# State-space phase: SyncE's u and lag stores ahead of its loads, and a second buffer for the lag kernels' load in place of the fourth unit buffer

## The chip, the cores and the metric

The kernel runs on one core of one Trainium2 chip. The metric is the device time of one execution in microseconds. The kernel before took 1748.19 us, the median of three runs (1745.48 to 1751.16).

## The reference

The kernel computes two blocks of a small model on 256 tokens of width 1024, in float32. The change lies in the second layer of the first block, a state-space mixer (S5) over 2048 channels, cut into 128 groups of 16 channels with 64 complex states each, forward and backward in time:

```
u = p.reshape(tokens, 128 groups, 16)            # p, z: the two halves of h @ s5_w_in
abar = exp(lam * dt);  bbar = ((abar - 1) / lam) * b;  cmat = c
h_t = abar * h_{t-1} + bbar u_t ;  y_t = Re(cmat h_t)     # both directions, first over the 256 context tokens
y = d * u + y_forward + y_backward
out = gelu(y) * sigmoid(gelu(y) @ glu_w + glu_b)          # then * silu(z) @ w_out, and a layer norm
```

## The kernel before

The state-space phase is the function s5_mixer. It works in chunks of 128 channels (8 groups), CT = 16 chunks, software-pipelined over steps n = 0 to 26. The recurrence is cut into pieces of CH = 8 tokens: states are carried from piece to piece by a scan, and inside a piece the effect of u on y is a small convolution, whose matrices (the "lag kernels") are worked out on the chip. In step n, TensorE (PE) does in this order:

- lag_kernels(n-9): ps_l from V and b (L1769 to L1778), then ScalarE copies it to lags (L1899).
- project(n): u of chunk n, 24 matmuls of 512 columns (L1745); from step 16 on a gate_half (24 of 256 columns) in place of it, and a second one at the end of the step. The weights come as "units" of 512 KB, which ScalarE and VectorE first split into a leading part and a rest (lead, L1858; rest, L1971).
- outputs(n-10): y from V and the states hs, and from the lag kernels T and u (L1794).
- the state matmuls of chunk n-2: ps_s from the 1 MB input weights W and the re-laid u, ub (L1841). ScalarE copies them into S (L1936 to L1938).

VectorE scans S in quads of four chunks (advance, L1982 to L1985), spread over steps n = 4q+6 to 4q+9; ScalarE's states() (L1878, L1879) then makes hs. GpSimd (POOL) makes V of a chunk (L1729 to L1731) once the outputs three chunks before are done (y_done), except for chunks 4, 6, 8, 10 and 12, whose V is loaded (quad_loads, L1611).

SyncE issues all of the phase's transfers, in program order, on one queue; a wait on SyncE stops everything behind it. Its loop over n does before:

1. unit load n+4 (512 KB, L1505), after rest(n); from step 16 on two units
2. W load of chunk n-1 (1 MB, L1509), after the state matmuls of chunk n-3
3. u store of chunk n-1 (256 KB, L1646), after u_kept
4. z and g stores and loads (L1650, L1655, L1659)
5. lag store of chunk n-9 (four DMAs of 30 KB, L1663), then b (L1597), cc (L1600) and every fourth step apow (L1606)
6. ub load of chunk n-1 (256 KB, L1680), after the u store has landed (u_stored): it reads u back in another layout
7. T load of chunk n-9 (512 KB, L1688), after the lag store has landed and after outputs(n-10) (y_done): it reads overlapping windows of the lag kernels, 1 KB each
8. V loads, tables, gate weights, and the small loads of the first steps

T has one buffer, half of the resident x (whose contents are spilled for the phase). Units have four buffers in the ring, u % 4. PE waits in outputs(k) for T_landed, in project for the unit (through rest_made), in the state matmuls for s5_w_landed and ub_landed. The DRAM side of the u store has 8 as its outermost count, that of the T and ub loads too, that of one lag store 16, that of the unit, W, b and cc loads 128.

Of the kernel before, what the change touches and what calls it, by code (L numbers as in the profile page):

```python
# [21 lines left out]
P = 128  # L22
DM = 1024
KT = DM // P
NL = 256
# [5 lines left out]
ET = E // P  # L31
# [35 lines left out]
class Core:  # L67


    def __init__(self, nc, ctx, d):  # L70
        self.nc, self.d = nc, d
        sb = lambda name, shape: ctx.enter_context(nc.sbuf_tensor(f"resident_{name}", shape, F32))
        self.ring = sb("ring", [P, 2, KT * NW])
        self.x = sb("x", [P, LT, DM])
        self.ident = sb("ident", [P, P])
        self.modT = sb("modT", [P, 2, 16, 2])
        self.eps = sb("eps", [P, 2])
        self.norm_g = sb("norm_g", [P, 4, KT])
        self.fold = sb("fold", [P, 2, KT])
        self.ms, self.rs = sb("ms", [P, LT, 2]), sb("rs", [P, LT])  # L80
        self.landed = [ctx.enter_context(nc.semaphore(f"weights_landed{s}")) for s in range(2)]
        many = lambda n, c: [ctx.enter_context(nc.semaphore(f"{n}{s}")) for s in range(c)]
        self.s5_unit_landed, self.s5_w_landed, self.gate_landed = many("s5_unit_landed", 4), many("s5_w_landed", 2), many("gate_landed", 4)
        self.q_stored = ctx.enter_context(nc.semaphore("q_stored"))
        self.tables_stored = ctx.enter_context(nc.semaphore("tables_stored"))
        self.spent = []
        self.used = [0, 0]
# [1074 lines left out]
CH = 8  # L1162
# [333 lines left out]
def s5_unit(core, u):  # L1496
    return core.ring[:, 0, (u % 4) * KT * P:(u % 4 + 1) * KT * P]

# [5 lines left out]
def s5_unit_load(core, sp, u):  # L1504
    sp.dma_start(s5_unit(core, u), core.d["s5_w"][u]).then_inc(core.s5_unit_landed[u % 4], 16)  # L1505

# [5 lines left out]
def s5_prefetch(core, sp):  # L1512

    for u in range(4):
        s5_unit_load(core, sp, u)
    for k in range(2):
        s5_weights_load(core, sp, k)
# [10 lines left out]
def s5_mixer(core, hparts, xc, low, wparts, gT):  # L1528
# [6 lines left out]
    with phase(core, "ssm") as ph:  # L1535
# [21 lines left out]
        vt = ph.sb("vt", [P, 512])  # L1557
        T = core.x[:, 0, :].rearrange("p (j m q) -> p j m q", j=4, q=2)
        yv = core.x[:, 1, :].rearrange("p (t m) -> p t m", t=CH)
# [9 lines left out]
        y_done, y_kept, turned, g_made, cleared, feed_made = [sem(n) for n in "y_done y_kept turned g_made cleared feed_made".split()]  # L1569
        lag_stored, T_landed, g_stored, z_stored, feed_in = [sem(n) for n in "lag_stored T_landed g_stored z_stored feed_in".split()]  # L1570
        ub_landed = [sem(f"ub_landed{s}") for s in range(3)]
# [14 lines left out]
        def windows(k):  # L1586

            return bass.AP(tensor=lagged.tensor, offset=lagged.offset + k * SG * CG * LAGW, ap=[[2 * SG, CH], [2 * LAGW, SG * 4], [1, 2 * P]])

        with ph.block() as block:  # L1590
            @block.sync
            def _(sp):
# [41 lines left out]
                for n in range(STEPS + 1):  # L1634
                    k, kl = n - OUT, n - LAG
                    for u in units(n):
                        if u + 4 < SsmUnits.UNITS:
                            sp.wait_ge(rest_made, u + 1)
                            s5_unit_load(core, sp, u + 4)
                    if n >= 3 and is_ct(n - 1):  # L1640
                        sp.wait_ge(s_done, 2 * (n - 2))
                        s5_weights_load(core, sp, n - 1)
                    if is_ct(n - 1):
                        sp.wait_ge(u_kept, n)
                        to = d["u"][n - 1]
                        sp.dma_start(bass.AP(tensor=to.tensor, offset=to.offset, ap=[[CH * NCH, CG], [CG * CH * NCH, SG], [1, CH * NCH]]), us[(n - 1) % 2][:]).then_inc(u_stored[(n - 1) % 2], 16)  # L1646
                    done = units(n - 1)
                    if done and done[0] >= CT:
# [7 lines left out]
                    if k in (6, 10):  # L1656
                        q = (k - 6) // 4
                        sp.wait_ge(g_made, 2 * (q + 1))
                        sp.dma_start(d["g"][4 * q:4 * q + 4].rearrange("j p n -> p j n"), gb[:]).then_inc(g_stored, 16)  # L1659
                    if is_ct(kl):  # L1660
                        sp.wait_ge(l_kept, kl + 1)
                        for j in range(4):
                            sp.dma_start(lagged[kl][:, j], lags[32 * j:32 * j + SG].rearrange("m w q -> m (w q)")).then_inc(lag_stored, 16)  # L1663
                        if kl + 2 < CT:
                            sp.wait_ge(l_done, kl + 1)
                            small_loads(kl + 2)
                        if kl + 4 < CT:
                            if kl not in LOADED:
                                sp.wait_ge(v_made, 2 * quads_made(kl))
                            c_load(kl + 4)  # L1670
                    if n >= BACK + 8 and (n - BACK - 8) % 4 == 0 and (n - BACK) // 4 < NQ:
                        sp.wait_ge(scanned, (n - BACK) // 4 - 1)
                        apow_load((n - BACK) // 4)
                    if is_ct(n - 1):
# [10 lines left out]
                    if is_ct(kl):  # L1685
                        sp.wait_ge(lag_stored, 64 * (kl + 1))
                        sp.wait_ge(y_done, kl)
                        sp.dma_start(core.x[:, 0, :].rearrange("p (j m) -> p j m", j=4), windows(kl)).then_inc(T_landed, 16)  # L1688
                    if kl == CT - 2:
                        for u in range(2):  # L1690
                            gate_load(core, sp, u)
                    if is_ct(k) and k + 3 in LOADED:
                        sp.wait_ge(y_done, k + 1)
                        quad_loads(k + 3)
                    if is_ct(k) and k % 4 == 3 and k // 4 + 2 < NQ:
                        sp.wait_ge(v_made, 2 * quads_made(k))
                        table_load(k // 4 + 2)
                    later_loads(n)
                sp.wait_ge(rest_made, SsmUnits.UNITS)
                for u in range(2, 4):  # L1700
                    gate_load(core, sp, u)
                sp.wait_ge(z_stored, 16 * (CT // 2))
# [32 lines left out]
            def _(pe):  # L1735
# [45 lines left out]
                def outputs(k):  # L1781
                    pe.wait_ge(hs_made, k + 1)
                    if k >= 4 and k % 2 == 0:
                        pe.wait_ge(y_kept, k // 2 - 1)
                    pe.wait_ge(T_landed, 16 * (k + 1))
                    pe.wait_ge(ul_made, k + 1)
                    for q in range(2):
                        r = 2 * k + q
                        bank, slot = ps_y[r % 8 // 4], r % 4
                        for src in range(3):  # L1790
                            for j in range(4):
                                lhs = ul[:, k % 9, 4 * q + j, :] if src == 2 else hs[:, src, (r % 8) * 4 + j, :]
                                rhs = T[:, j, :, q] if src == 2 else V[:, r % RING, src, j, :]
                                last = nc.tensor.matmul(bank[32 * j:32 * j + 32, slot, :], lhs, rhs, start=src == 0, stop=src == 2)  # L1794
                    last.then_inc(y_done, 1)
# [21 lines left out]
                for n in range(STEPS):  # L1817
# [3 lines left out]
                    if n < CT:  # L1821
                        pe.wait_ge(core.s5_unit_landed[n % 4], 16 * (n // 4 + 1))
                        pe.wait_ge(u_kept, n)
                        project(n, ps_u[:], slice(0, NTOK), u_done)
# [24 lines left out]
            def _(act):  # L1849
                sc = nc.scalar  # L1850

                def lead(u):
                    act.wait_ge(core.s5_unit_landed[u % 4], 16 * (u // 4 + 1))
                    if u >= 2:
                        act.wait_ge(u_done, min(u - 1, CT))
                        if u - 1 > CT:
                            act.wait_ge(z_done, u - 1 - CT)
                    sc.activation(w_lead[:, u % 2], s5_unit(core, u).rearrange("p (k c) -> p k c", k=KT), ACT.Copy).then_inc(lead_made, 1)  # L1858
# [34 lines left out]
                for n in range(STEPS):  # L1893
                    k, kl = n - OUT, n - LAG
                    if is_ct(kl):
                        if kl:
                            act.wait_ge(lag_stored, 64 * kl)
                        act.wait_ge(l_done, kl + 1)
# [1241 lines left out]
def build(nc, d, out, start=0):  # L3140

    for name, shape in (("mod", [2, 2, DM]), ("s5_q", [SN, CH, 2, P]), ("s5_p", [P, NQ, CH, 2, QG]), ("s5_a", [P, NQ, LEVELS, 3, QG]),
                        ("s5_bb", [P, 2, SN, SG]), ("s5_W", [CT, P, 4, WB * 2 * P]), ("s5_V", [2 * len(EarlyQuads.TILES), P, 2, 4 * P]), ("x1", [P, LT, DM]), ("u", [CT, SG, CG, CH * NCH]),
                        ("lags", [CT, SG, 4, LAGW * 2]), ("g", [ET, P, NL]), ("z", [ET, P, NL])):
        d[name] = nc.dram_tensor(name + "_scratch", shape, F32, kind="Internal").ap()
# [158 lines left out]
```

## Time and profile before

| | us |
|---|---|
| median of three runs (lowest, highest) | 1748.19 (1745.48, 1751.16) |
| span of the profiled execution, first to last instruction | 1745.1 |
| the profiled execution's own time beside its span | not given by the page |
| PE busy in the span | 1558.8 (89%) |
| state-space phase in the trace, about | 562 to 923 |

The page is of one profiled execution. Times in the views are microseconds from the start of the span. An engine's "idle before" is the time it waited ahead of an instruction, with the releaser that came last by the profile; where it says "issue", the profile shows no engine that released it, which for a wait on a DMA's semaphore is the usual form. The granted clock of TensorE is given as a share of full speed (1.00 is 2.4 GHz, 0.50 is 1.2 GHz, a mean over a stretch lies between). The DMA share is the mean busy share of the core's 16 DMA engines.

### The profile page before, as it was taken

How to read it: one execution, taken by the hardware profiler on the slowest of the kernel's cores; microseconds unless marked ns; L12 is line 12 of the kernel's file. 1: busy time of each engine (PE TensorE's matmuls, PEld its weight loads, DVE VectorE, ACT ScalarE, POOL GpSimd, SP SyncE). 2: the span in 40 equal slices, each digit the busy share in tenths (PEclk: the TensorE clock that was granted, in tenths of full speed). 3: DMA queues.
4: the chain of work that ended last, by engine and by line, in shares of the span. 5: the costliest groups of instructions: out<-in, count | busy, mean ns of one | idle time of the engine just before them, and what ended most of it. 6: DMA issues, size and time to landing. Idle time of an engine off the chain costs nothing. (4 is left out here: it accounts for less than half of the span.)

```text
span 1745.1 us, 28068 instructions
## 1 busy us (share of the span) xinstructions
PE 1558.8 (89%) x11286; PEld 1331.2 (76%) x11286; DVE 975.0 (56%) x1271; ACT 806.6 (46%) x1096; POOL 661.1 (38%) x507
## 2 busy tenths in 40 slices
PE   3799999799798888888759988898999999899998
PEld 0378888588686777778658976677999967689997
DVE  6444422488744267556825636564666655546665
ACT  2522222455414557576554434554544454455452
POOL 0088986599698923445751013211000010110000
PEclk9889999899899989889978998888999999899999
DMA  9966666455535567777756545313454433245441
GB/s 390 426 247 224 236 228 229 140 195 192 200 113 197 158 196 209 200 242 191 206 140 254 186 165 206 145 49 146 194 216 170 167 111 136 85 166 217 194 167 49
DMA packets 118649, 330.75 MB, mean 190 GB/s; under 512 B 31732, under 2 KB 72052, under 8 KB 102280
## 3 DMA queue, kind: packets, MB, share of 16 engines
q1 hardware_dynamic: 115670, 303.67, 49.6%
q10 hardware_dynamic: 2868, 25.54, 4.0%
q8 instruction: 78, 1.28, 0.3%
q14 instruction: 33, 0.27, 0.0%
HBM read 290.55 MB, written 38.62 MB: 189 GB/s over the span
## 5 line engine op out<-in xcount | busy, mean ns | idle before, releaser
L3010 PE MATMUL ffn_ps<-ffn_x_lead,w_lead 128*128 128x256 f32 x672 | 188.4, 280 | 1.1 <-DVE w_rest L3089 1.1
L3010 PE MATMUL ffn_ps<-ffn_x_lead,w_rest 128*128 128x256 f32 x672 | 188.6, 281 | 0.0
L3010 PE MATMUL ffn_ps<-ffn_x_rest,w_lead 128*128 128x256 f32 x672 | 188.4, 280 | 0.0
L401 POOL TENSOR_TENSOR w_rest<-resident_ring,w_lead 128x2048 fp32r<-128x2048 f32 x7 | 32.1, 4580 | 402.1 <-ACT w_lead L397 211.7
L3089 DVE TENSOR_TENSOR w_rest<-resident_ring,w_lead 128x2048 fp32r<-128x2048 f32 x42 | 96.1, 2292 | 83.8 <-ACT w_lead L3054 83.8
L365 PE MATMUL qkvz_ps<-qkvz_w_lead,h_lead 128*128 128x512 f32 x320 | 125.7, 393 | 5.4 <-POOL h_rest L646 5.4
L3010 PEld LDWEIGHTS ffn_ps<-ffn_x_lead,w_lead 128*128 128x128 f32 x672 | 126.1, 188 | 2.2 <-issue 1.5
L3010 PEld LDWEIGHTS ffn_ps<-ffn_x_rest,w_lead 128*128 128x128 f32 x672 | 126.4, 188 | 0.7
L3010 PEld LDWEIGHTS ffn_ps<-ffn_x_lead,w_rest 128*128 128x128 f32 x672 | 126.3, 188 | 0.0
L365 PE MATMUL qkvz_ps<-qkvz_w_rest,h_lead 128*128 128x512 f32 x320 | 125.4, 392 | 0.0
L365 PE MATMUL qkvz_ps<-qkvz_w_lead,h_rest 128*128 128x512 f32 x320 | 125.4, 392 | 0.0
L282 DVE TENSOR_TENSOR qkvz_w_rest<-resident_ring,qkvz_w_lead 128x2048 fp32r<-128x2048 f32 x20 | 50.7, 2534 | 124.2 <-ACT qkvz_w_lead L276 124.2
L282 DVE TENSOR_TENSOR w_rest<-resident_ring,w_lead 128x2048 fp32r<-128x2048 f32 x33 | 78.3, 2375 | 73.5 <-ACT w_lead L276 73.1
L1729 POOL TENSOR_TENSOR ssm_V<-ssm_ptab,ssm_cc 128x512 f32<-128x512 f32 x44 | 59.2, 1346 | 140.0 <-PE ssm_ps_y L1794 137.2
L276 ACT ACTIVATE qkvz_w_lead<-resident_ring 128x2048 fp32r<-128x2048 f32 x20 | 38.5, 1924 | 150.2 <-PE qkvz_ps L365 148.0
L1971 DVE TENSOR_TENSOR w_rest<-resident_ring,w_lead 128x1024 fp32r<-128x1024 f32 x32 | 46.9, 1469 | 107.1 <-ACT w_lead L1858 106.9
L276 ACT ACTIVATE w_lead<-resident_ring 128x2048 fp32r<-128x2048 f32 x33 | 63.2, 1914 | 89.6 <-PE odd_ps L365 29.9
L3054 ACT ACTIVATE w_lead<-resident_ring 128x2048 fp32r<-128x2048 f32 x42 | 80.1, 1912 | 50.7 <-PE ffn_ps L3010 50.6
L1418 POOL TENSOR_TENSOR resident_x<-xc,resident_x 128x512 f32<-128x512 f32 x64 | 99.1, 1548 | 5.0
L1745 PE MATMUL ssm_ps_u<-h_lead,w_lead 128*128 128x512 f32 (+1 forms) x256 | 93.8, 366 | 4.6 <-issue 2.4
L1745 PE MATMUL ssm_ps_u<-h_lead,w_rest 128*128 128x512 f32 (+1 forms) x256 | 88.9, 347 | 2.6 <-issue 2.6
L1745 PE MATMUL ssm_ps_u<-h_rest,w_lead 128*128 128x512 f32 (+1 forms) x256 | 89.2, 348 | 0.0
(518 smaller groups left out, 4531.6 us busy)
## 6 DMA issues: line engine op xcount, KB each, us to landing
resident_ring<-in_ffn_gu SPq DMA_DIRECT2D x22, 2048.0 KB, 9.0
ffn_wd<-in_ffn_down SPq DMA_DIRECT2D x22, 1024.0 KB, 4.8
resident_ring<-in_ada_w SPq DMA_DIRECT2D x8, 2048.0 KB, 13.6
xc<-s_q_scratch SPq DMA_DIRECT2D x128, 128.0 KB
resident_x<-in_s_bT SPq DMA_DIRECT2D x64, 256.0 KB
resident_ring<-in_attn_w_in ACTq DMA_DIRECT2D x8, 2048.0 KB, 10.1
s_W_scratch<-resident_x SPq DMA_DIRECT2D x64, 256.0 KB, 3.5
resident_ring<-in_s_w SPq DMA_DIRECT2D x32, 512.0 KB, 6.1
```

The source lines that it names most:

```text
L276: self.core.nc.scalar.activation(self.w[0][j], self.core.tile(r)[:, j * HK:(j + 1) * HK, :], ACT.Copy).then_inc(self.lead_made, 1)
L282: self.core.nc.vector.tensor_tensor(self.w[1][j], self.core.tile(r)[:, j * HK:(j + 1) * HK, :], self.w[0][j].bitcast(F32), ALU.subtract).t ...
L365: last = nc.tensor.matmul(bank(parity, t), self.lhs[x][:, half * HK + k, t * P:(t + 1) * P], self.w[w][j][:, k, :], start=(half, k, x, w) ...
L401: self.core.nc.gpsimd.tensor_tensor(self.slots[1][0], self._raw(r), self.slots[0][0].bitcast(F32), ALU.subtract).then_inc(self.rest_made, 1)
L1418: g.tensor_tensor(b, q(0), b, ALU.mult).then_inc(self.scaled, 1)
L1729: g.tensor_tensor(v, power(c), coef(0), ALU.mult)
L1745: last = nc.tensor.matmul(out, w[:, s, k, :], hparts[x][:, k, cols], start=k == 0 and x == 0 and w is w_lead, stop=k == KT - 1 and w is w_ ...
L1971: v.tensor_tensor(w_rest[:, u % 2], raw, w_lead[:, u % 2].bitcast(F32), ALU.subtract).then_inc(rest_made, 1)
L3010: last = nc.tensor.matmul(ps[s][f][:, m, :], w_part[w][m][:, k, f * P:(f + 1) * P], x_part[x][:, k, :], start=(k, w, x) == (0, 0, 0), stop ...
L3054: nc.scalar.activation(w_part[0][m], raw(s, m), ACT.Copy).then_inc(w_lead_made, 1)
L3089: v.tensor_tensor(w_part[1][m], raw(s, m), w_part[0][m].bitcast(F32), ALU.subtract).then_inc(w_rest_made, 1)
```

## The change

SyncE's loop now runs in this order: u store; from step 16 on the two unit loads; z and g; W load; lag store; ub load; T load; below step 16 the unit load; b, cc and apow; V loads and tables; gate weights. The four lag stores of 16 partitions each become one of all 128 partitions (twice the bytes), and the scratch tensor gets twice the rows, so that the windows read by T are the same. T has two buffers: half of x, and what was the fourth unit buffer; T(k) waits for outputs(k-2) in place of outputs(k-1). Units have three buffers, and each is asked for three units ahead in place of four. T_landed becomes two semaphores. At the end gate load 3, which overwrites the second T buffer, waits for outputs(14).

```diff
 def s5_unit(core, u):
-    return core.ring[:, 0, (u % 4) * KT * P:(u % 4 + 1) * KT * P]
+    return core.ring[:, 0, (u % 3) * KT * P:(u % 3 + 1) * KT * P]
...
-        T = core.x[:, 0, :].rearrange("p (j m q) -> p j m q", j=4, q=2)
+        T_raw = [m.rearrange("p (j m) -> p j m", j=4) for m in (core.x[:, 0, :], core.ring[:, 0, 3 * KT * P:4 * KT * P])]
+        T = [m.rearrange("p j (m q) -> p j m q", q=2) for m in T_raw]
...
                 for n in range(STEPS + 1):
                     k, kl = n - OUT, n - LAG
-                    for u in units(n):
-                        if u + 4 < SsmUnits.UNITS:
-                            sp.wait_ge(rest_made, u + 1)
-                            s5_unit_load(core, sp, u + 4)
-                    if n >= 3 and is_ct(n - 1):
-                        sp.wait_ge(s_done, 2 * (n - 2))
-                        s5_weights_load(core, sp, n - 1)
                     if is_ct(n - 1):
                         sp.wait_ge(u_kept, n)
                         to = d["u"][n - 1]
...
+                    if n >= CT:
+                        for u in units(n):
+                            if u + 3 < SsmUnits.UNITS:
+                                sp.wait_ge(rest_made, u + 1)
+                                s5_unit_load(core, sp, u + 3)
...
+                    if n >= 3 and is_ct(n - 1):
+                        sp.wait_ge(s_done, 2 * (n - 2))
+                        s5_weights_load(core, sp, n - 1)
                     if is_ct(kl):
                         sp.wait_ge(l_kept, kl + 1)
-                        for j in range(4):
-                            sp.dma_start(lagged[kl][:, j], lags[32 * j:32 * j + SG].rearrange("m w q -> m (w q)")).then_inc(lag_stored, 16)
-                        if kl + 2 < CT:
-                            sp.wait_ge(l_done, kl + 1)
-                            small_loads(kl + 2)
-                        if kl + 4 < CT:
-                            if kl not in LOADED:
-                                sp.wait_ge(v_made, 2 * quads_made(kl))
-                            c_load(kl + 4)
-                    if n >= BACK + 8 and (n - BACK - 8) % 4 == 0 and (n - BACK) // 4 < NQ:
-                        sp.wait_ge(scanned, (n - BACK) // 4 - 1)
-                        apow_load((n - BACK) // 4)
+                        of = lagged[kl]
+                        sp.dma_start(bass.AP(tensor=of.tensor, offset=of.offset, ap=[[LAGW * 2, 4], [4 * LAGW * 2, 2 * SG], [1, LAGW * 2]]),
+                                     lags[:].rearrange("m w q -> m (w q)")).then_inc(lag_stored, 16)
                     if is_ct(n - 1):
                         sp.wait_ge(u_stored[(n - 1) % 2], 16 * ((n - 1) // 2 + 1))
...
                     if is_ct(kl):
-                        sp.wait_ge(lag_stored, 64 * (kl + 1))
-                        sp.wait_ge(y_done, kl)
-                        sp.dma_start(core.x[:, 0, :].rearrange("p (j m) -> p j m", j=4), windows(kl)).then_inc(T_landed, 16)
-                    if kl == CT - 2:
-                        for u in range(2):
-                            gate_load(core, sp, u)
+                        sp.wait_ge(lag_stored, 16 * (kl + 1))
+                        if kl >= 2:
+                            sp.wait_ge(y_done, kl - 1)
+                        sp.dma_start(T_raw[(kl + 1) % 2], windows(kl)).then_inc(T_landed[kl % 2], 16)
+                    if n < CT:
+                        for u in units(n):
+                            if u + 3 < SsmUnits.UNITS:
+                                sp.wait_ge(rest_made, u + 1)
+                                s5_unit_load(core, sp, u + 3)
+                    if is_ct(kl):
+                        if kl + 2 < CT:
+                            sp.wait_ge(l_done, kl + 1)
+                            small_loads(kl + 2)
+                        if kl + 4 < CT:
+                            if kl not in LOADED:
+                                sp.wait_ge(v_made, 2 * quads_made(kl))
+                            c_load(kl + 4)
+                    if n >= BACK + 8 and (n - BACK - 8) % 4 == 0 and (n - BACK) // 4 < NQ:
+                        sp.wait_ge(scanned, (n - BACK) // 4 - 1)
+                        apow_load((n - BACK) // 4)
                     if is_ct(k) and k + 3 in LOADED:
                         sp.wait_ge(y_done, k + 1)
                         quad_loads(k + 3)
...
+                    if kl == CT - 2:
+                        for u in range(2):
+                            gate_load(core, sp, u)
...
-                for u in range(2, 4):
-                    gate_load(core, sp, u)
+                gate_load(core, sp, 2)
+                sp.wait_ge(y_done, CT - 1)
+                gate_load(core, sp, 3)
...
-("lags", [CT, SG, 4, LAGW * 2])
+("lags", [CT, 2 * SG, 4, LAGW * 2])
```

## Rows read from the trace of the kernel before

**Rows 1.** The page, its first line.
```profile
span 1745.1 us, 28068 instructions
```

**Rows 2.** Windows: length, busy us of PE, PEld, DVE, ACT, POOL, clock, DMA share, GB/s.
```profile
595.65:657.50 61.85, 56.23 (x313) 49.15 (x311) 31.18 (x46) 38.79 (x62) 24.34 (x19) 0.89 0.64 207
...
679.56:797.41 117.85, 103.51 (x1569) 92.19 (x1569) 69.85 (x78) 78.17 (x116) 64.69 (x47) 0.87 0.78 221
...
846.75:898.31 51.56, 36.58 (x680) 33.75 (x680) 25.70 (x26) 27.28 (x36) 49.66 (x36) 0.88 0.54 132
```

**Rows 3.** Waits of PE, 540 to 930 us: total us, times, longest.
```profile
PE ssm_ps_y L1794 <- issue: 25.0, 6, 10.4
PE ssm_ps_y L1794 <- ACT ssm_hs L1879: 11.7, 2, 6.9
PE ssm_ps_l L1769 <- issue: 9.7, 3, 4.9
...
PE ssm_ps_s L1841 <- issue: 5.6, 4, 2.6
```

**Rows 4.** Timeline of PE, lead-in, state matmuls of chunks 0, 1 and 6: start, length.
```profile
586.58 3.68 PE L1841 MATMUL ssm_ps_s<-ssm_ub,resident_ring 128*128 128x64 f32 x32
...
595.65 3.68 PE L1841 MATMUL ssm_ps_s<-ssm_ub,resident_ring 128*128 128x64 f32 x32
...
653.89 3.68 PE L1841 MATMUL ssm_ps_s<-ssm_ub,resident_ring 128*128 128x64 f32 x32
```

**Rows 5.** Waits of SyncE's queue, 540 to 930 us.
```profile
SPq L1680 <- DMA u_scratch<-ssm_us: 90.4, 15, 8.7
```

**Rows 6.** Timeline of SyncE's queue, lead-in: u store and the ub load behind it.
```profile
574.05 0.62 SPq L1646 DMA_DIRECT2D u_scratch<-ssm_us  x1
578.07 0.60 SPq L1680 DMA_DIRECT2D ssm_ub<-u_scratch  x1
...
605.32 0.63 SPq L1646 DMA_DIRECT2D u_scratch<-ssm_us  x1
612.68 0.62 SPq L1680 DMA_DIRECT2D ssm_ub<-u_scratch  x1
```

**Rows 7.** Timeline of SyncE's queue, 671 to 790 us: T loads, one u store, its ub load.
```profile
671.17 0.58 SPq L1688 DMA_DIRECT2D resident_x<-lags_scratch  x1
...
685.13 0.96 SPq L1688 DMA_DIRECT2D resident_x<-lags_scratch  x1
...
688.73 0.59 SPq L1646 DMA_DIRECT2D u_scratch<-ssm_us  x1
...
699.29 0.61 SPq L1680 DMA_DIRECT2D ssm_ub<-u_scratch  x1
...
734.26 0.59 SPq L1688 DMA_DIRECT2D resident_x<-lags_scratch  x1
...
789.16 0.59 SPq L1688 DMA_DIRECT2D resident_x<-lags_scratch  x1
```

**Rows 8.** DMA view, 605 to 612 us, 40 slices: unit and W (middle).
```profile
DMA  8799212389999999876789979999944254455551
GB/s 230 243 310 234 70 23 94 164 360 451 398 398 421 398 468 421 281 328 234 328 374 421 468 328 515 421 374 421 375 187 187 94 222 164 187 211 199 211 199 59
```

**Rows 9.** DMA view, 879.5 to 887.5 us: T(13) by itself, then a z store.
```profile
DMA  0000023052555556555459999556595400000005
```

**Rows 10.** Timeline of ACT: the copy of the first lag kernels.
```profile
660.21 0.60 ACT L1899 ACTIVATE ssm_lags<-ssm_ps_l 128x480 f32<-128x480 f32 x1
```

**Rows 11.** Timeline of SyncE's queue, tail: lag store and T load of chunk 15.
```profile
902.92 1.72 SPq L1663 DMA_DIRECT2D lags_scratch<-ssm_lags  x4
...
905.88 0.60 SPq L1688 DMA_DIRECT2D resident_x<-lags_scratch  x1
```

**Rows 12.** Timeline of PE, tail: outputs(15).
```profile
914.31 1.08 PE L1794 MATMUL ssm_ps_y<-ssm_V,ssm_hs 128*32 128x128 f32 x16 [10.35 <-issue]
```

**Rows 13.** Timeline of SyncE's queue: units 28 and 29 before, 27 and 28 after.
```profile
839.78 1.47 SPq L1505 DMA_DIRECT2D resident_ring<-in_s_w  x2
```

**Rows 14.** Timeline of ACT: unit 27 converted.
```profile
850.27 1.06 ACT L1858 ACTIVATE w_lead<-resident_ring 128x1024 fp32r<-128x1024 f32 x1
```

More of the change, by code:

```diff
@@ L82, in __init__ @@
         many = lambda n, c: [ctx.enter_context(nc.semaphore(f"{n}{s}")) for s in range(c)]
-        self.s5_unit_landed, self.s5_w_landed, self.gate_landed = many("s5_unit_landed", 4), many("s5_w_landed", 2), many("gate_landed", 4)
+        self.s5_unit_landed, self.s5_w_landed, self.gate_landed = many("s5_unit_landed", 3), many("s5_w_landed", 2), many("gate_landed", 4)
         self.q_stored = ctx.enter_context(nc.semaphore("q_stored"))
@@ L1504, in s5_unit_load @@
 def s5_unit_load(core, sp, u):
-    sp.dma_start(s5_unit(core, u), core.d["s5_w"][u]).then_inc(core.s5_unit_landed[u % 4], 16)
+    sp.dma_start(s5_unit(core, u), core.d["s5_w"][u]).then_inc(core.s5_unit_landed[u % 3], 16)
 def s5_weights_load(core, sp, k):
@@ L1512, in s5_prefetch @@
 def s5_prefetch(core, sp):
-    for u in range(4):
+    for u in range(3):
         s5_unit_load(core, sp, u)
@@ L1569, in s5_mixer @@
         y_done, y_kept, turned, g_made, cleared, feed_made = [sem(n) for n in "y_done y_kept turned g_made cleared feed_made".split()]
-        lag_stored, T_landed, g_stored, z_stored, feed_in = [sem(n) for n in "lag_stored T_landed g_stored z_stored feed_in".split()]
+        lag_stored, g_stored, z_stored, feed_in = [sem(n) for n in "lag_stored g_stored z_stored feed_in".split()]
+        T_landed = [sem(f"T_landed{s}") for s in range(2)]
         ub_landed = [sem(f"ub_landed{s}") for s in range(3)]
@@ L1586, in windows @@
         def windows(k):
-            return bass.AP(tensor=lagged.tensor, offset=lagged.offset + k * SG * CG * LAGW, ap=[[2 * SG, CH], [2 * LAGW, SG * 4], [1, 2 * P]])
+            return bass.AP(tensor=lagged.tensor, offset=lagged.offset + k * 2 * SG * CG * LAGW, ap=[[2 * SG, CH], [2 * LAGW, SG * 4], [1, 2 * P]])
         with ph.block() as block:
@@ L1784, in outputs @@
                         pe.wait_ge(y_kept, k // 2 - 1)
-                    pe.wait_ge(T_landed, 16 * (k + 1))
+                    pe.wait_ge(T_landed[k % 2], 16 * (k // 2 + 1))
                     pe.wait_ge(ul_made, k + 1)
@@ L1792, in outputs @@
                                 lhs = ul[:, k % 9, 4 * q + j, :] if src == 2 else hs[:, src, (r % 8) * 4 + j, :]
-                                rhs = T[:, j, :, q] if src == 2 else V[:, r % RING, src, j, :]
+                                rhs = T[(k + 1) % 2][:, j, :, q] if src == 2 else V[:, r % RING, src, j, :]
                                 last = nc.tensor.matmul(bank[32 * j:32 * j + 32, slot, :], lhs, rhs, start=src == 0, stop=src == 2)
@@ L1821, in _ @@
                     if n < CT:
-                        pe.wait_ge(core.s5_unit_landed[n % 4], 16 * (n // 4 + 1))
+                        pe.wait_ge(core.s5_unit_landed[n % 3], 16 * (n // 3 + 1))
                         pe.wait_ge(u_kept, n)
@@ L1852, in lead @@
                 def lead(u):
-                    act.wait_ge(core.s5_unit_landed[u % 4], 16 * (u // 4 + 1))
+                    act.wait_ge(core.s5_unit_landed[u % 3], 16 * (u // 3 + 1))
                     if u >= 2:
@@ L1896, in _ @@
                         if kl:
-                            act.wait_ge(lag_stored, 64 * kl)
+                            act.wait_ge(lag_stored, 16 * kl)
                         act.wait_ge(l_done, kl + 1)
@@ L3143, in build @@
                         ("s5_bb", [P, 2, SN, SG]), ("s5_W", [CT, P, 4, WB * 2 * P]), ("s5_V", [2 * len(EarlyQuads.TILES), P, 2, 4 * P]), ("x1", [P, LT, DM]), ("u", [CT, SG, CG, CH * NCH]),
-                        ("lags", [CT, SG, 4, LAGW * 2]), ("g", [ET, P, NL]), ("z", [ET, P, NL])):
+                        ("lags", [CT, 2 * SG, 4, LAGW * 2]), ("g", [ET, P, NL]), ("z", [ET, P, NL])):
         d[name] = nc.dram_tensor(name + "_scratch", shape, F32, kind="Internal").ap()
```

## Prediction

> **What bounds the kernel now.** I read the page first, for the span: 1745.1 us in one profiled execution [rows 1]. The page gives no time around that span; the three timed runs have a median of 1748.19 (1745.48 to 1751.16), 3.1 us above it. I make the sum in the span and carry it over to the median.
>
> Second, the table by stretches [rows 2]. The change touches only the state-space phase, about 562 to 923 us. In its lead-in (595.65 to 657.50) PE is busy 56.23 of 61.85 us at a granted clock of 0.89; in the lag-kernel stretch (679.56 to 797.41) 103.51 of 117.85 us at 0.87, with a DMA share of 0.78. So PE is the engine that runs most, but idle time and a lowered clock leave room: 56.23 x 0.89 = 50 us and 103.51 x 0.87 = 90 us are the least that PE could do there. From 846.75 to 898.31 POOL is busy 49.66 of 51.56 us: it builds V for chunks 13, 14 and 15, and lag_kernels(15) waits for the last. That stretch keeps its length, whatever SyncE does.
>
> Third, what ended PE's idle time [rows 3]. "issue" stands where only a DMA semaphore can be meant: 25.0 us in six waits ahead of the outputs (T_landed), 5.6 us in four ahead of the state matmuls (ub_landed). The 11.7 us behind ssm_hs are the scan's and the 9.7 us ahead of ssm_ps_l mostly POOL's; neither is touched.
>
> Fourth, SyncE's queue. It loses 90.4 us in 15 waits for its own u store [rows 5]. The store sits behind the unit load and the 1 MB weights load: with nothing large ahead it takes 574.05 to 578.07 = 4.0 us until the dependent load can be issued, in the lead-in 605.32 to 612.68 = 7.4 us [rows 6], in the next stretch 688.73 to 699.29 = 10.6 us [rows 7]. As SyncE works in order, all later transfers wait too.
>
> **Part 1: u store first, unit load last (lead-in).** Removed from in front of the store: a wait for rest_made, one 512 KB load, a wait for s_done and one 1 MB load. The store is now queued as soon as ScalarE has made u; I price store to ub issue at 4.0 us in place of 7.4 or more. Nothing is queued behind a new wait here: u_kept was waited for at the same place in time. The ub load goes behind the weights load now, but is wanted a step and a half later. A step without a wait lasts 586.58 to 595.65 = 9.07 us [rows 4], and SyncE's own cycle, 4.0 us of store and some 2 us for its other issues, fits into it. From 595.65 to 653.89 five steps take 58.2 us [rows 4]; five of 9.07 are 45.4, an excess of 12.9. Lower bound of the gain: the waits alone, 5.6 us [rows 3]; upper: 12.9. PE at full clock would give 61.85 - 50 = 11.8 [rows 2]. I take 11, near the upper end, because the clock falls in the very steps with a wait. After it PE is the bound there.
>
> **Part 2: two buffers for T, and the wait on y_done one chunk looser (lag-kernel stretch).** Before, T(k) was issued after outputs(k-1); now after outputs(k-2), so the 25.0 us could go. But what ends last in this stretch is not that wait. Four issues of T follow each other from 671.17 to 734.26, 63.1 us, or 15.8 a cycle; T(1) is issued at 685.13, the u store queued behind it at 688.73 is not known to be stored until 699.29, and T follows it [rows 7]. The cycle is the content of the queue: T, unit, weights, u store, ub. The bytes stay, so a second buffer alone shortens nothing once the queue is the bound. All seven cycles (671.17 to 789.16) take 118.0 us, 16.9 each, since PE at its low clock held up the last three.
>
> What changes in the cycle: SyncE now waits for lag_stored instead of u_stored ahead of T. The lag store, and the small b and cc loads of the chunk before, come into the cycle. The new store moves 240 KB where four of 30 KB moved 120 KB. No row shows its form, so bounds. The DMA share tells how wide a transfer runs: with unit and weights loads it is 9 tenths and more at about 400 GB/s [rows 8]; with T by itself 5 to 6 tenths at some 165 GB/s, though it too covers 128 partitions [rows 9]. T's DRAM pattern has 8 as its outermost count, the weights' 128, the new store's 4. Carried on, 4 means a quarter of the engines and half T's rate, 82 GB/s: 245,760 bytes take 3.0 us. If it runs wide, 0.6 us at 400 GB/s. The two rows fit the outer counts, so I stay near the first, and take 2.6 us, as its pieces are 1.9 KB against T's 1 KB.
>
> The Trainium skill, page "DMA: Bandwidth & Descriptors", section "Why a DMA increments its semaphore by 16 and not by 1", says how many engines a copy gets: the largest number up to 16 that divides the slowest dimension of both sides. By it T gets 8, the new lag store 4, the old ones 16; the share rows agree for 8 and for 128. The same page's "Rules for kernel authors" say to coalesce many small transfers into a large one, which speaks for the new store: by that rule the store would cost 0.6 us and the stretch go the way of the second case below.
>
> Cycle: 15.8 + 2.6 (lag store) + 1.0 (256 KB of b and cc: 0.65 us at 400 GB/s, 1.6 at T's 165) - 1.6 (an estimate: issue and start-up between u stored at 699.29 and the first data of ub, now covered by ub behind the lag store; between 0 and 2.1) - 0.6 (an estimate: the weights are issued later and mix less with T; between 0 and 1.2) = 17.2. Seven: 120.4 us, 2.4 more than 118.0. Against that T(0) starts earlier: the first lag kernels are copied at 660.8 [rows 10], and a store needs 4.0 us till its dependent load when quiet [rows 6], of which 256 KB at T's rate are 1.6; with 2.6 instead it is 5.0. So T(0) goes out at about 665.8 and lands 8.4 us later, as the last one did (issue at 905.88, use at 914.31 [rows 11, 12]), at 674.2. Seven cycles on, that is 5.4 us before the 679.56 at which outputs(0) began. PE stalls more evenly, and I add 2 us for its clock behind the last one. Together 2.4 - 5.4 + 2 = -1.0. Bounds: a cycle of 14.0 (the shortest shown, 671.17 to 685.13 [rows 7]) would let PE set the pace: from 117.85 to about 97 (90 plus what ScalarE and POOL cost), a gain of 21; one of 20 us gives 140 - 118 - 5.4 + 2 = +19.
>
> **What is moved past what.** small_loads, c_load and apow_load with their waits (l_done, v_made, scanned) now stand behind T and ub: 1.6 us of issues and, where V is late, POOL leave T's path; counted in the cycle through b and cc alone. Their users come two steps later or more: 0. Three issues a chunk go with the single lag store, under 1.5 us of SyncE, hidden as SyncE waits anyway. The wait of quad_loads for outputs(k) stays in every other step and now holds back the next u store instead of a unit load; u is made at about that time, 0 to 2 us, inside the u path's step and a half. ScalarE's wait for lag_stored before it overwrites the lags is for a store a whole step old: 0.
>
> **Part 3: three unit buffers.** In steps below 16 the load is asked for two steps ahead, 18 us or more, and T, as large and made of smaller pieces, lands in 8.4: nothing. From step 16 on units come in pairs; the odd one is now asked for one pair later. The tightest is unit 27: asked for at 839.78, converted at 850.27 [rows 13, 14], 10.5 us against at most T's 8.4. Cost 0; without that cover up to 3 us at a step, hidden in part by the POOL chain.
>
> **Part 4: the tail.** lag store(15) starts at 902.92, T(15) at 905.88 [rows 11]: 3.0 us. outputs(15) starts at 914.31 after a wait of 10.35 [rows 12]. The new store takes the 5.0 of above. So +2 (0, if wide, to +3), on the path. Gate load 3 waits for outputs(14), which is over by then: 0.
>
> **Sum.** -11 - 1.0 + 2 = -10.0: span 1735.1, median 1738.2, say 1738.
>
> **The cases.** What a measurement can tell from no change is 0.3%, 5.2 us.
>
> 1. Forecast, the lead-in's gain stays and the queue binds the rest: 1738, own range 1730 to 1744. Chance 0.44.
> 2. The queue keeps up (lag store wide, or little of it in the cycle), PE becomes the bound and is held by POOL's V and the scan: 11 + 10 to 21 = 21 to 32 gained, near 1723. For it: DMA share 0.78, not 1 [rows 2]. Against: u_stored is late in every cycle. Chance 0.19.
> 3. The lead-in's gain is given back by longer cycles: at 18.6 us a cycle, 7 x 18.6 = 130 = 118 + 5.4 + 11 - 2 - 2, nothing is left: 1748. For it: every term that I added could be larger while loads mix. Chance 0.25.
> 4. Slower: the narrow lag store in front of T in each of the seven cycles. Its engines are those that T needs too. Price: each us on the cycle is 7 us; it decides from 18.6 us a cycle. At 20: 140 - 118 - 5.4 + 2 + 2 - 11 = +10, 1758. Against: it needs 1.4 us a cycle more than I count, so a lag store that is 4 us on the path, or 5.4 for a cycle of 20. Chance 0.12.
>
> That the stores aren't first is excluded: on SyncE the program order is the issue order.
>
> Faster by over 0.3% holds case 1 without its edge and case 2: 0.62. Same: case 3 and that edge: 0.26. Slower: 0.12. Range 1721 to 1753: it holds cases 1 to 3 but for their ends.
>
> **What would show it.** Lead-in: ub issued about 4 us after each u store, no idle time ahead of the state matmuls, and lag_kernels(0) near 646 to 648. Lag stretch: T issues 17 us apart, SyncE waiting on lag_stored where it waited on u_stored, waits of 2 to 4 us ahead of the outputs remaining; if these are gone, case 2. The lag store's data: 2.6 us at a DMA share of about a quarter; if half a us, part 2 is wrong. Tail: T(15) issued 5 us after its lag store. The prediction is wrong if lag_kernels(0) doesn't come 8 us earlier, or the seven cycles take less than 112 or more than 128 us.

## The result, and the profile after

The changed kernel takes 1751.35 us (median of 19 runs, 1742.96 to 1756.91), the kernel before in the same runs 1746.26 (19 runs too; one of them took 3855 us, which hardly moves the median). The ratio is 1.0038 with a 95% interval of 1.0022 to 1.0055: slower by about 6.6 us (the medians themselves lie 5.1 us apart), where 1738 was forecast. A second set of runs gave 1.0034 (1.0012 to 1.0057; e9 below). The profiled execution took 1747.88 us.

The page's first line, and three windows that answer to [rows 2] (columns as there: length, busy us of PE, PEld, DVE, ACT, POOL, clock, DMA share, GB/s).

```profile
span 1746.1 us, 28018 instructions
...
594.33:647.35 53.02, 51.84 (x325) 46.27 (x323) 29.64 (x41) 39.81 (x63) 24.57 (x19) 1.00 0.77 240
667.86:796.50 128.64, 103.41 (x1569) 92.25 (x1570) 76.76 (x90) 79.54 (x118) 68.89 (x48) 0.85 0.76 213
848.15:899.95 51.80, 36.84 (x681) 34.06 (x681) 25.04 (x26) 27.50 (x36) 49.69 (x36) 0.89 0.56 145
```

The lead-in is full now: PE works 51.84 of 53.02 us at full clock, and lag_kernels(0) starts at 647.35 in place of 657.50. The POOL stretch has kept its 52 us. What is lost lies between them, in the lag-kernel stretch: the same 1569 matmul instructions, with the same 103.4 us of PE busy, took 117.85 us before and 128.64 now. At 796.50, where outputs(7) start, all but 0.9 of the 10 us are gone (797.41 before).

What PE waits for, and what SyncE's queue waits for (total us, times, longest; [rows 3] and [rows 5] before).

```profile
PE ssm_ps_y L1806 <- issue: 37.8, 7, 13.4
PE ssm_ps_y L1806 <- ACT ssm_hs L1891: 12.0, 2, 7.2
PE ssm_ps_l L1781 <- issue: 8.7, 2, 4.9
...
SPq L1683 <- DMA lags_scratch<-ssm_lags: 96.9, 15, 9.8
SPq L1674 <- DMA u_scratch<-ssm_us: 84.2, 16, 8.6
```

The state matmuls' wait for ub is gone, and the outputs' wait for T has grown from 25.0 to 37.8 us in spite of its second buffer. SyncE's wait for the u store fell only from 90.4 to 84.2 us, and the wait for the lag store, here 96.9 us, was before

```profile
SPq L1688 <- DMA lags_scratch<-ssm_lags: 16.1, 10, 4.5
```

About a third of the 96.9 us (34.0, in seven waits) falls between 655 and 790 us, in the seven cycles; 62.9 us lie behind them, where the scan and POOL hold PE too. A third wait is new, and on ScalarE:

```profile
ACT ssm_b_fw L1874 <- DMA ssm_b_all<-s_bb_scratch: 27.4, 6, 8.8
```

Behind T and the unit load, b lands too late for ScalarE, which copies it ahead of u. The next lines are SyncE's timeline, to be read against [rows 6, 7, 11]: a u store and its ub load in the lead-in, the lag store and T of chunk 0, the T loads of chunks 4 and 7, and the tail.

```profile
602.55 0.61 SPq L1641 DMA_DIRECT2D u_scratch<-ssm_us  x1
608.34 0.61 SPq L1674 DMA_DIRECT2D ssm_ub<-u_scratch  x1
...
650.76 0.55 SPq L1666 DMA_DIRECT2D lags_scratch<-ssm_lags  x1
659.17 0.60 SPq L1683 DMA_DIRECT2D resident_ring<-lags_scratch  x1
...
728.62 0.59 SPq L1683 DMA_DIRECT2D resident_ring<-lags_scratch  x1
788.82 0.59 SPq L1683 DMA_DIRECT2D resident_x<-lags_scratch  x1
...
904.56 0.55 SPq L1666 DMA_DIRECT2D lags_scratch<-ssm_lags  x1
911.17 0.60 SPq L1683 DMA_DIRECT2D resident_x<-lags_scratch  x1
```

From T(0) to T(7) it is 129.65 us, 18.5 a cycle (before: 16.9). The first four take 17.4 each (before: 15.8), the last three 20.1 (before: 18.3). The DMA view from 904.5 to 912 us (slices of 0.19 us) shows how few engines the lag store uses: behind the gate weights the busy share drops to 2 tenths for 2.5 us.

```profile
DMA  9999979958448081555423222222222210000000
```

### The profile page after: what moved, and what is told of

Same layout as the page of the kernel before. It is cut to its first block and busy times, and to the rows that moved or that the text cites. A ratio compares the mean times of both kernels' runs of the same rounds, so it can differ in the third digit from the quotient of the medians.

```text
span 1746.1 us, 28018 instructions
## 1 busy us (share of the span) xinstructions
PE 1552.3 (89%) x11286; PEld 1327.1 (76%) x11286; DVE 974.2 (56%) x1271; ACT 806.5 (46%) x1096; POOL 663.3 (38%) x507
## 6 DMA issues: line engine op xcount, KB each, us to landing
resident_ring<-in_attn_w_in ACTq DMA_DIRECT2D x8, 2048.0 KB, 10.3
```

## The experiments

All ratios are to the kernel before, from five rounds on one chip for each group of four (e1 to e4, e5 to e8, e9 to e12), with 95% intervals; 0.1% is 1.7 us. Each kernel has one trace, and two traces of the changed kernel differ (lag store to T takes 12.9 us in the mean of chunks 1 to 7 in the first, 13.5 in e9), so differences of a few tenths between traces say nothing. Two names run through the experiments. Theory A: the narrow lag store (4 as outermost count) in front of T. Theory B: b, cc and apow behind T and the unit load.

| | ratio | interval |
|---|---|---|
| changed kernel | 1.0038 | 1.0022 to 1.0055 |
| e1 new order in the lead-in only | 0.9909 | 0.9878 to 0.9939 |
| e2 changed, b back ahead of T | 0.9992 | 0.9965 to 1.0018 |
| e3 changed, wide lag store | 0.9924 | 0.9894 to 0.9954 |
| e4 before, narrow lag store | 1.0044 | 1.0017 to 1.0071 |
| e5 changed, e2 and e3 together | 0.9898 | 0.9863 to 0.9932 |
| e6 changed, T waits for outputs(k-1) | 1.0047 | 1.0020 to 1.0074 |
| e7 before, new order in all steps | 0.9894 | 0.9865 to 0.9924 |
| e8 e5, late units behind T too | 0.9951 | 0.9928 to 0.9974 |
| e9 changed again | 1.0034 | 1.0012 to 1.0057 |
| e10 e7, narrow lag store | 1.0002 | 0.9973 to 1.0032 |
| e11 e7, b behind T | 0.9945 | 0.9922 to 0.9968 |
| e12 e7, three unit buffers | 0.9887 | 0.9852 to 0.9923 |

**e1, the lead-in alone.**

```diff
-  unit load; W load; u store          # n < 9, before
+  u store; W load; ...; ub load; unit load
```

> The kernel before with one edit: below step 9 the u store is issued ahead of the W load, and the unit load behind the ub load. From step 9 on everything is as before. Theory P (the prediction's part 1 holds by itself, and the lag-kernel stretch gives none of it back): ratio to before 0.994, about 1736 us, and no idle time of PE ahead of the state matmuls of chunks 1 to 6. Rival G (whatever the lead-in gains is lost again, because the queue and POOL set the stretch behind it): ratio 0.998 to 1.000, with the outputs from chunk 7 on at the times of the kernel before.

It is 0.9% faster, 16 us with an interval of 11 to 21, more than the 10 that were expected (0.994 lies just outside the interval). Theory P holds and G is out: the stretch behind the lead-in gives nothing back by itself.

**e2, b ahead of T again.** small_loads, c_load, apow_load and their waits stand right behind the lag store.

> The changed kernel with b, cc and apow (and their waits) put back to right behind the lag store, ahead of ub and T. Theory B (the b load behind T and the unit lands late, ScalarE waits for it 24.6 us between 655 and 800 us, and with ScalarE u is late, its store, and the next T): ScalarE's wait for b is gone, the T issues are 17 us apart or less, 7 x 1.5 = 10 us faster than the changed kernel, about 1741 us, ratio to before 0.997. Theory A (it is the narrow lag store in front of T): the T cycle stays at 18.5 us or grows by the 1.0 us of b and cc, ratio 1.004 to 1.008.

0.46% faster than the changed kernel, some 8 us; the two intervals just miss each other, but this one overlaps that of e9. ScalarE's wait for b is gone and the T cycle is 17.5 us. B is real, but too small: e2 is only level with the kernel before.

**e3, the store made wide.**

```diff
-  sp.dma_start(AP(lagged[kl], [[LAGW*2, 4], [4*LAGW*2, 2*SG], [1, LAGW*2]]), lags[:])
+  for j in range(4):
+      sp.dma_start(lagged[kl][:, j], lags[32*j:32*j + 2*SG])
```

> The changed kernel with its one lag store split into four of 32 partitions each: the same 240 KB, but with 32 as the outermost count of each in place of 4. Theory A (narrow lag store on T's path): 2.6 us of data become 0.6, 2.0 us less in each of seven cycles and 2 in the tail, 16 us faster than the changed kernel, about 1735, ratio to before 0.994. Theory B (ScalarE's wait for b): at most 2 to 4 us faster, ratio 1.001 to 1.003, T issues still 18 us apart, the tail 2 us shorter.

1.1% faster than the changed kernel, 20 us, for the same bytes and three more issues: what differs is how wide they run. A holds. Its T cycle is 16.95 us.

**e4, the narrow store in the old order.** In the kernel before, the four stores of 16 partitions (120 KB) become the changed kernel's one store (240 KB).

> The kernel before with one edit: its four lag stores of 16 partitions become the changed kernel's one store of 128 partitions with 4 as its outermost count. All is issued in the old order. Theory A: 2 us more in each of the seven cycles and in the tail, ratio 1.006 to 1.009. Theory B: the u store and its wait come behind it anyway, and only the tail feels it: ratio 1.000 to 1.002.

+0.44%, 8 us (3 to 12): between the two theories. From lag store to T it is 12.5 us in the mean of chunks 1 to 7, where the kernel before has 10.3, so the store does cost its 2 us there; but the T cycle is 17.7 in place of 16.9, so that more than half of them is hidden in the cycle, and where isn't shown. In the tail T(15) goes out 9.8 us behind its lag store (before: 3.0); e10 below takes that up.

**e5, both.**

> The changed kernel with both edits of e2 and e3: b, cc and apow back to right behind the lag store, and the lag store as four of 32 partitions. If the narrow store and the late b are two separate losses, their ratios multiply: 0.9924 x 0.9992 / 1.0038 = 0.988, about 1725 us. If both sit on the same cycle (a T later by the one hides the wait for b of the other), the gain over e3 is under 0.2%: ratio 0.991 to 0.993.

0.9898 lies between the two expectations, its interval (0.9863 to 0.9932) holds both, and so it doesn't decide between them. But it is level with e1: what the second T buffer and the later steps' order are worth beside the lead-in is too small for these intervals, under some 0.4%.

**e6, the second T buffer unused.**

```diff
-  if kl >= 2: sp.wait_ge(y_done, kl - 1)
+  sp.wait_ge(y_done, kl)
```

> The changed kernel, but T(k) waits for outputs(k-1) as the kernel before does, so that the second T buffer is never filled ahead. Theory Q (the queue sets the T cycle, the second buffer buys nothing: outputs(k-1) end 3 us or more before T(k) is issued): ratio 1.003 to 1.005, as the changed kernel. Rival D (the second buffer does help): T issues later by the time from one to the other, slower than the changed kernel by over 0.3%: ratio over 1.007.

1.0047 against 1.0038, with a T cycle of 18.4 us against 18.5: the runs favour Q, though the upper end of the interval, 1.0074, just reaches D. The trace says more. In the seven cycles the wait for outputs(k-1) is never the one that ends last ahead of a T, so there the second buffer has nothing to give. From T(8) on it ends last eight times:

```profile
SPq L1681 <- PE ssm_ps_y L1805: 37.1, 8, 8.9
```

Q's condition (outputs(k-1) over 3 us before T(k)) fails there, but in that stretch PE waits for the scan and for POOL's V as well, and no difference is seen in the time.

**e7, the order alone.** The four stores of 16 partitions, b behind them, one T buffer, four unit buffers; only the loads are reordered.

> The kernel before with the new order of u store, W load and unit load in all steps (u store first, W load ahead of the lag store, unit load behind T below step 16), and nothing else: its four narrow-free lag stores of 16 partitions, b, cc and apow behind them, one T buffer, four unit buffers. Against e1, which has the new order below step 9 only. Theory Q (behind step 9 the queue holds the same bytes, so the order there is worth nothing): ratio 0.989 to 0.993, the T cycle 16.5 us. Rival U (u store first and the unit last also shorten the later cycles): ratio under 0.987, T cycle 15.5 or less. If it is above 0.995, the new order itself costs in the later steps.

0.9894, level with e1, with a T cycle of 16.35 us: Q again. This version beats both kernels; e1, e5 and e12 do too and can't be told apart from it.

**e8, the late units behind T.** From step 16 on the two unit loads too stand behind T.

> e5, and from step 16 on the two unit loads also stand behind T (in the changed kernel and in e5 they stand ahead of the W load and the lag store). Theory E (in step 16 1 MB of units and 1 MB of W stand ahead of the lag store, and T(7) is late by what the units take): T(7) goes out 2.5 us earlier, 0.1 to 0.2% faster than e5. Rival F (with three unit buffers the units are then late for the gates): slower than e5 by 0.2% or more, with idle time of PE ahead of the gate matmuls.

T(7) comes earlier (the last three cycles are 17.0 us in place of e5's 17.8), as E says, but ScalarE then waits for units, 0.7 us in e5 and 39.2 us here, and the kernel is 0.5% slower than e5 (the two intervals overlap by 0.04%): F.

```profile
ACT w_lead L1863 <- DMA resident_ring<-in_s_w: 39.2, 6, 10.0
```

**e9, the changed kernel again.**

> The changed kernel itself, once more, on the chip of e10 to e12. 1.002 to 1.006 of before, with a first-four T cycle of 17.4 us, a last-three cycle of 20.1, and a lag store of chunk 15 that is 6.6 us ahead of its T.

Ratio and T cycles (17.4 and 20.4) came out as expected, the tail did not: 11.1 us from lag store(15) to T(15), where the first trace of the same kernel has 6.6. The next experiment bears on that.

**e10, the changed kernel's lag store in the new order.** It is narrow and moves 240 KB in place of 120; width alone is what e3 tested.

> e7 (new order, old buffers, b behind the lag store) with the changed kernel's narrow lag store in place of the four of 16 partitions, and nothing else. Theory A (alone it costs what e2 to e5 differed by, 0.94%): ratio 0.997 to 1.001, T cycles 1.3 us longer than e7's 16.35. Rival H (in the old order it cost 0.44%, e4, and the place does not matter): ratio 0.993 to 0.995.

1.08% slower than e7, 19 us, and the intervals are far apart. A holds, H is out. From each lag store to its T it is 12.6 us in the mean of chunks 1 to 7, where e7 has 10.6: the 2.0 us by which the narrow store was priced. Windows from outputs(0) to (3) and (3) to (7), first e7, then e10, then the changed kernel:

```profile
665.51:710.84 45.33, 41.75 (x649) 36.16 (x649) 34.43 (x42) 33.53 (x54) 30.45 (x20) 0.92 0.85 220
710.84:777.48 66.64, 54.59 (x921) 49.30 (x921) 41.29 (x47) 48.33 (x71) 40.24 (x29) 0.93 0.84 243
```

```profile
666.38:715.97 49.59, 43.81 (x649) 38.43 (x650) 37.07 (x42) 34.42 (x55) 31.58 (x21) 0.90 0.75 214
715.97:789.19 73.22, 55.78 (x920) 50.45 (x921) 38.07 (x49) 46.68 (x68) 36.19 (x28) 0.89 0.78 233
```

```profile
667.86:720.53 52.67, 42.37 (x648) 36.81 (x649) 38.26 (x43) 31.68 (x48) 34.52 (x24) 0.91 0.76 205
720.53:796.50 75.97, 61.03 (x921) 55.44 (x922) 38.50 (x47) 47.85 (x70) 34.37 (x25) 0.81 0.76 219
```

The lengths are to be read: 45.3, 49.6, 52.7 and 66.6, 73.2, 76.0 us. The narrow store makes 10.8 of the 16.7 us between e7 and the changed kernel here. It does not weigh the same in all cycles: from e7 to e10 the first four grow by 0.6 us each (15.7 to 16.3), the last three by 2.1 (17.2 to 19.3). In the tail it does more than its 2 us. SyncE's queue, e10, from lag store(14) to T(15):

```profile
884.86 0.55 SPq L1664 DMA_DIRECT2D lags_scratch<-ssm_lags  x1
890.48 0.59 SPq L1690 DMA_DIRECT2D resident_x<-lags_scratch  x1
891.11 0.98 SPq L1525 DMA_DIRECT2D resident_ring<-in_s_glu_w  x2
...
896.13 0.55 SPq L1664 DMA_DIRECT2D lags_scratch<-ssm_lags  x1
906.94 0.59 SPq L1690 DMA_DIRECT2D resident_x<-lags_scratch  x1
```

and e7, T(14), the gate weights, lag store(15), T(15):

```profile
874.35 0.60 SPq L1689 DMA_DIRECT2D resident_x<-lags_scratch  x1
874.99 0.99 SPq L1525 DMA_DIRECT2D resident_ring<-in_s_glu_w  x2
...
885.64 2.65 SPq L1664 DMA_DIRECT2D lags_scratch<-ssm_lags  x4
889.53 0.60 SPq L1689 DMA_DIRECT2D resident_x<-lags_scratch  x1
```

lag_kernels(15) come when POOL has V(15), T(14) comes late by what the stores have cost. So the last lag store, issued 11.3 us behind T(14) in e7, comes only 5.7 us behind it in e10, while T(14) and 2 MB of gate weights still stand ahead of it in the queue, and its T goes out 10.8 us after it in place of 3.9. The two traces of the changed kernel fit this: 9.5 us behind T(14) and 6.6 to T(15) in the first, 5.4 and 11.1 in e9. Lag store(14), with nothing large ahead, needs 5.6 us. The DMA view of e10 from 895 to 907 (slices of 0.3 us) shows the last one's 2 tenths only where the gate weights have run out, 8 us after its issue:

```profile
DMA  9795989979468999999999754554532222222200
```

**e11, b behind T alone.**

> e7 with b, cc and apow and their waits moved behind T and the unit load, and nothing else. Theory B (b is late for ScalarE by itself, 20 us of waits or more in five or six waits, and u and its store with it): 0.25 to 0.5% slower than e7, ratio 0.992 to 0.995. Rival (with a lag store that is over in time, T is early enough to hide it): ratio 0.988 to 0.991, and under 10 us of ScalarE waiting for b.

0.51% slower than e7 (the intervals just touch, the sign is that of e2 against the changed kernel). ScalarE waits for b as follows, between the two limits that were set:

```profile
ACT ssm_b_fw L1869 <- DMA ssm_b_all<-s_bb_scratch: 17.2, 6, 6.1
```

**e12, three unit buffers.**

> e7 with three unit buffers in place of four, each asked for three units ahead, and T still in its one buffer. Theory C (the prediction: cost nothing): ratio 0.988 to 0.991. Rival (from step 16 on the units come one pair later, and the step from outputs(7) to outputs(8) takes 24 to 25 us, as in e2, e3, e5, e6 and e8, in place of 20): 4 to 5 us slower than e7, ratio 0.992.

0.9887, level with e7. The step from outputs(7) to (8) did take 23.0 us in place of 20.3, but nothing of it is seen at the end: theory C. There are only six runs of it, and the interval's upper end, 0.9923, just reaches the rival's 0.992.

Together: e7's 0.9894, plus 1.08% for the narrow store, plus 0.51% for b, plus nothing for the buffers, is 1.005; the changed kernel has 1.0038 (1.0022 to 1.0055).

## Why the prediction was wrong

**Part 1 was right.** Each u store has its ub load 4.0 us behind it in the first two steps and 5.6 to 6.4 in the rest of the lead-in, no state matmul waits, and lag_kernels(0) start 10.2 us earlier, of the 11 taken. By itself the edit is worth 16 us (11 to 21), e1, above the prediction's upper bound of 12.9 in the middle of its interval, not in all of it.

**The price of the narrow store was right.** 2.6 us of data were counted: the trace has 128 pieces of 1.9 KB, 79 ns each, on four engines, 2.5 us from the first to the last, and e10 against e7 gives 2.0 us more from lag store to T than the old stores. The Trainium skill, "DMA: Bandwidth & Descriptors", section "Why a DMA increments its semaphore by 16 and not by 1", gives four engines for an outermost count of 4; the share of 2 tenths agrees. Of the same page's "Rules for kernel authors" in the Trainium skill, the one to coalesce small transfers led the wrong way here, as one store in place of four cost 20 us (e3); the one to put a size that is a multiple of 16 outermost, so that all engines are used, is what the runs bear out.

**The first four T cycles were right, the last three were not.** 17.2 us were forecast for all seven, and the first four took 17.4. The step that failed is the base of the other three: the four cycles of 15.8 [rows 7] were carried on to all seven, on the ground that "PE at its low clock held up the last three" (18.3 each), with 2 us as the whole allowance for the clock. They took 20.1: 8.6 us more than forecast. On the base of 18.3 the prediction's own 1.4 us of change would have given 19.7. From outputs(3) to (4), (4) to (5) and (6) to (7) the windows are, before:

```profile
727.65:747.46 19.81, 19.81 (x216) 17.61 (x216) 7.72 (x7) 10.84 (x13) 1.58 (x1) 0.62 0.82 244
747.46:767.83 20.37, 17.63 (x250) 15.49 (x249) 13.33 (x10) 13.03 (x21) 17.12 (x12) 0.83 0.69 204
781.50:797.41 15.91, 14.29 (x242) 13.44 (x241) 6.45 (x14) 11.58 (x18) 12.75 (x11) 0.94 0.83 235
```

and after:

```profile
720.53:740.27 19.74, 19.74 (x217) 17.54 (x217) 6.03 (x5) 12.97 (x18) 1.03 (x1) 0.63 0.79 219
740.27:760.54 20.27, 17.52 (x249) 15.41 (x249) 13.25 (x10) 13.02 (x21) 17.22 (x12) 0.83 0.76 218
774.47:796.50 22.03, 13.36 (x241) 12.67 (x242) 13.52 (x24) 11.29 (x17) 16.12 (x12) 0.85 0.79 256
```

The first two steps have the same length in both kernels. In the first PE has no idle time at all and runs at 0.62 to 0.63, behind a wait for T(3) of 5.41 us before and 5.03 after. In e7, where outputs(3) wait 1.7 us in all, the same step has the full clock and is 4.4 us shorter (the second one takes 20.1 us there too):

```profile
710.84:726.25 15.41, 13.45 (x216) 11.40 (x217) 9.06 (x7) 11.23 (x15) 6.29 (x5) 1.00 0.75 199
```

But the low clock of that step is not what makes the last three cycles long. The same step in e6 and in e1:

```profile
717.77:733.76 15.99, 13.03 (x216) 11.30 (x217) 9.23 (x9) 13.33 (x19) 0.00 (x0) 1.00 0.74 189
```

```profile
710.41:728.97 18.56, 18.56 (x217) 16.64 (x217) 6.95 (x6) 10.25 (x13) 1.89 (x2) 0.68 0.82 238
```

e6 has the full clock there, and its last three cycles take 20.1 us, as in the changed kernel; e1 has 0.68, and they take 17.9. Nor does the wait alone set the clock: in e9 outputs(3) waited 5.86 us and the step ran at 0.89. So the prediction's ground for leaving the 18.3 aside is not borne out. In all 14 traces the last three cycles are longer than the first four, by 1.4 us (e7) to 3.1 (e5). Part of it is the last one: T(7) was late, 13.4 us behind its lag store, with two units and 1 MB of W ahead of the store, and PE was idle for 8.67 us; with the units behind T (e8) the last three are 0.8 us shorter each than in e5. What makes up the rest isn't shown.

**T(0)'s head start was 3.4 us too large.** 5.0 us were taken from lag store to T, as if in a quiet queue; it took 8.4, as the ub load and what stood before it were still moving. Even quiet it is 5.6 (e10, lag store(14)).

**"Their users come two steps later or more: 0" was wrong.** ScalarE copies b ahead of u in every step, and waited 27.4 us for it; that cost 0.5%, 8 to 9 us (e2, e11), for a term put at nothing. It is partly inside the cycles above (18.5 us a cycle, 17.5 in e2), so it isn't a further term of the sum; that the first four cycles came out right with this term missing is in part luck.

**The second T buffer and three unit buffers: nothing measurable, where 0 was forecast** (e6, e12).

**The tail** was forecast with +2. From outputs(7) to the next phase it took 6.3 us more than before (131.7 against 125.4), of which 3.7 lie behind lag_kernels(15): T(15) went out 6.6 us behind its lag store, not 5.0, for the gate weights in front of it (11.1 us in e9, so this term varies from one execution to the next).

**The sum.** Forecast -10.0 in the span. outputs(7) came 11.1 us later than it gives: 8.6 from the last three cycles, 0.6 from the first four, 4.4 from T(0) (3.4 and some 1 from a lead-in gain of 10.2), less the 2 that had been allowed for the clock, which add up to 11.6. The part behind outputs(7) adds 4.3. That is 15 of the 16.6 us between forecast and result. This sum holds for the phase in two traces: at its end the changed kernel is 5.3 us behind, while the two spans differ by only 1.0 us, as the unchanged rest of the program took 4.3 us less in that execution.

The experiments give the same miss without traces. e1 and e7 have the new order without the rest, and the changed kernel is 23 and 25 us slower than they are; everything beyond the lead-in was forecast at +1.0. The price of the narrow store is not where that went wrong. With 0.6 us in its place the prediction's working gives 18 us less (14 in the cycles, 2 at T(0), 2 in the tail), 28 us gained; e3 gained 13 and e5, with b back as well, 18. So some 10 us are missing without the narrow store and with b in its old place; by the traces they belong to the base of the cycles, T(0) and the tail. The other 5 of e3 are those of b.

Case 4 had the place and the mechanism: the narrow store in front of T, decisive from 18.6 us a cycle, where 18.5 and 18.7 were measured. Its chance of 0.12 was too small, because the forecast stood 1.4 us from its point and every term in between was an estimate; the prediction's own mark for being wrong, more than 128 us for seven cycles, was met with 129.65.

What makes the last three cycles longer than the first four, in every version, was not tested by itself.

## What to carry to other kernels

When many small transfers are joined into one, look at the outermost count of both sides before counting bytes: four stores with 32 outermost made the kernel 20 us faster than one store of the same bytes with 4. A second buffer bought nothing that could be measured while the queue that fills it was late anyway; first find what the queue waits for. Where a stretch repeats a cycle, take its base from all the steps to be forecast: the last three differed from the first four here, and leaving them out cost the most. And before a load is moved behind others as "not yet needed", look up its first reader in the program order of that engine: here it stood ahead of the work that feeds the whole cycle.

## What the runs showed of the hardware

The same 240 or so matmul instructions of the step from outputs(7) to (8) kept PE busy for 13.3 us at full clock (e11), 15.5 at 0.84 (e7) and 20.5 at 0.70 (e5), in this order:

```profile
784.84:802.98 18.14, 13.34 (x240) 12.63 (x241) 14.17 (x17) 11.82 (x17) 0.76 (x1) 1.00 0.75 238
```

```profile
777.48:797.78 20.30, 15.52 (x240) 14.47 (x240) 10.49 (x10) 10.51 (x14) 0.00 (x0) 0.84 0.82 222
```

```profile
780.12:805.40 25.28, 20.49 (x241) 19.36 (x241) 12.01 (x13) 10.37 (x14) 0.00 (x0) 0.70 0.69 190
```

And the narrow store did not slip past the wide transfers issued before it: in e10 the last lag store's data begin 8 us after its issue, when T(14) and 2 MB of gate weights are through. The Trainium skill, "DMA: Bandwidth & Descriptors", section "Queues, rings and completion order", says that each engine takes its descriptors in the order of its ring; the DMA row of e10 agrees.
